# Position biases added by VectorE, and 128-fold bias tables, in a three-block fp32 transformer kernel

## The reference, cut to what matters

```python
# block 1 (one layer): gated linear attention + block attention + convolutional FFN
proj = rmsnorm(x) @ w_in                     # qa ka va ra a_lr | qb kb vb | gates
oa = rmsnorm(gla_chunked(qa, ka, va, log_sigmoid(a_lr @ w_lr_up + b_forget) / 16)) * g * silu(ra)
logits = qb @ kb.T / 8 + rel_bias[t5_bucket(q_pos - k_pos)]      # 8 heads of 64
ob = softmax(where(k_pos <= q_pos, logits, -inf)) @ vb
mixed = g_a * (oa @ w_branch_gla) + g_b * (ob @ w_branch_moba)   # g = sigmoid(gates)
x = x + mixed @ w_out;  x = x + conv_swiglu(rmsnorm(x))
# block 2: stick-breaking attention and pooling, attention on a memory, then
logits = rmsnorm(x) @ w_router + b_router    # 32 experts
top4 = top_k(logits, 4); gates = softmax(top4)
x = x + sum over the 4 experts e of gate_e * (clamped_swiglu(h @ w1[e] + b1[e]) @ w2[e] + b2[e])
# block 3, two layers: l0 = sparse + differential attention with a T5 bias; l1 = the last:
logits = q @ k.T / 8 + table[clip(q_pos - k_pos)]                # 16 heads of 64
masked to the own chunk of 64 tokens and those before it; softmax; @ v
# each layer also: two half-step SwiGLU FFNs, attention on a memory; at the end rmsnorm
```

## Time and profile before

| | |
|---|---|
| median of three runs | 3231.62 us |
| the profiled execution | 3234.32 us, span 3232.5 us |
| PE busy | 3057.5 us (95%) |
| PEld busy | 2186.9 us (68%) |
| DVE busy | 781.9 us (24%) |
| ACT busy | 514.7 us (16%) |
| POOL busy | 12.5 us |
| DMA | 723.01 MB, mean 224 GB/s |

### The profile page before, as it was taken

The page is one execution under the profiler, slowest core; times in us unless marked ns, Lnnn a source line. Parts: engine busy times, 40 slices in busy tenths (PEclk is TensorE's granted clock), DMA queues, the critical chain, the costliest instruction groups (busy, mean ns, idle before and its releaser), DMA issues.

```text
span 3232.5 us, 34397 instructions
## 1 busy us (share of the span) xinstructions
PE 3057.5 (95%) x14190; PEld 2186.9 (68%) x14190; DVE 781.9 (24%) x1766; ACT 514.7 (16%) x1014; POOL 12.5 (0%) x21
## 2 busy tenths in 40 slices
PE   7999999999899998989988999989999999989999
PEld 5788888768443433433433888767888888857887
DVE  1131441332211111111111311454210210443210
ACT  2120320121111111111111100123200100132100
POOL 0000000000000000000000000000000000000000
PEclk9999999999899999999999999999999999998999
DMA  7333444323699999999999344532344444532341
GB/s 281 115 123 130 182 157 156 133 102 110 256 429 428 429 428 429 428 429 428 428 429 428 141 156 161 189 119 79 131 150 146 173 150 145 200 117 79 142 148 62
DMA packets 52217, 723.01 MB, mean 224 GB/s; under 512 B 5692, under 2 KB 5692, under 8 KB 8336
## 3 DMA queue, kind: packets, MB, share of 16 engines
q1 hardware_dynamic: 48672, 705.73, 54.7%
q0 software_dynamic: 3440, 15.74, 1.4%
HBM read 720.32 MB, written 1.12 MB: 223 GB/s over the span
## 4 chain that ended last, share of the span: by engine, by line
PE 79%; DMA 17%; DVE 2%; ACT 1%; issue 1%; SPq 0%; ACTq 0%; POOL 0%; DVEq 0%; POOLq 0%
PE ps L518 66%; DMA sb_a<-stream 9%; DMA sb_weights<-stream 8%; PE ps L1104 5%; PE ps L1126 4%; PE ps L1046 2%; PE ps L1081 2%; PE ps L777 1%; DVE sb_squares L1656 0%; ACT sb_squares L1346 0%; DVE sb_a L2176 0%; ACT sb_o L1278 0%; ACT sb_tr L1278 0%; ACT sb_ex L1346 0%; PE ps L1141 0%
## 5 line engine op out<-in xcount | busy, mean ns | idle before, releaser
L518 PE MATMUL ps<-sb_h,sb_weights 128*128 128x256 f32 x5328 | 1167.7, 381 | 29.1 <-DMA sb_weights<-stream 17.7
L518 PEld LDWEIGHTS ps<-sb_h,sb_weights 128*128 128x128 f32 x5328 | 1013.7, 191 | 173.2 <-issue 29.9
L1104 PE MATMUL ps<-sb_weights,sb_k 128*64 128x512 f32 x1792 | 461.8, 609 | 30.3 <-DMA sb_weights<-stream 26.7
L518 PE MATMUL ps<-sb_a,sb_weights 128*128 128x256 f32 x2016 | 438.9, 380 | 3.2 <-DVE sb_a L1910 3.2
L518 PEld LDWEIGHTS ps<-sb_a,sb_weights 128*128 128x128 f32 x2016 | 383.8, 191 | 56.3 <-DVE sb_a L1910 3.6
L1104 PEld LDWEIGHTS ps<-sb_weights,sb_k 128*64 128x64 f32 x1792 | 144.0, 140 | 316.9 <-issue 280.3
L1126 PE MATMUL ps<-sb_weights,sb_k 128*64 128x512 f32 x768 | 236.6, 614 | 52.7 <-DMA sb_a<-stream 28.9
L2070 DVE TENSOR_TENSOR sb_v<-ps,sb_small 128x256 f32<-128x256 f32 x128 | 48.4, 420 | 666.6 <-PE ps L1071 666.6
L1126 PEld LDWEIGHTS ps<-sb_weights,sb_k 128*64 128x64 f32 x768 | 72.4, 141 | 193.7 <-issue 193.7
L518 PE MATMUL ps<-sb_o,sb_weights 128*128 128x256 f32 x768 | 172.1, 386 | 7.9 <-DVE sb_o L1658 4.2
L1752 DVE TENSOR_TENSOR sb_ex<-ps,sb_rstd 128x512 f32<-128x512 f32 x88 | 60.9, 692 | 482.6 <-PE ps L518 482.4
(11 more groups left out here) (282 smaller groups left out, 1889.1 us busy)
## 6 DMA issues: line engine op xcount, KB each, us to landing
sb_weights<-stream SPq DMA_DIRECT2D x303, 2048.0 KB, 12.4
sb_a<-stream SPq DMA_DIRECT2D x32, 2048.0 KB, 18.3
sb_a<-tables POOLq DMA_DIRECT2D x2, 2048.0 KB, 17.8
sb_a<-tables POOLq DMA_DIRECT2D x2, 1536.0 KB, 15.2
sb_a<-tables POOLq DMA_DIRECT2D x2, 1024.0 KB, 10.7
sb_h<-mem POOLq DMA_DIRECT2D x2, 1024.0 KB, 5.1
sb_small<-small SPq DMA_DIRECT2D x1, 1390.0 KB, 9.4
sb_x<-x SPq DMA_DIRECT2D x1, 1024.0 KB, 4.8
```

Of the source, the lines that this page charges most:

```text
L518: ins = pe.matmul(out, lhsT, rhs, start=start, stop=stop, skip_group_check=skip)
L1104: ins = pe.matmul(ps[own[e], :], XG[:, k * PAIR + e * LOT:k * PAIR + (e + 1) * LOT], w[e][:, k * 512:(k + 1) * 512], start=k == 0, stop=k ...
```

## The change

1. *Biases by VectorE* (`added`, for `moba` and `band`): TensorE's bias matmuls are left out. DVE adds the bias tile from `A` to the PSUM logits, writes the sum to `ex(h)`, and takes the maximum there; this add frees the bank. ScalarE's exponentials run in place. DVE waits for the turning of head h-4, ScalarE no longer frees a bank but raises a semaphore of its own.
2. *Tables*: tables 0 and 2 are stored 128 times over (`wide_tables`), by a DMA whose source repeats each partition's row; they are loaded with a row step one less than a row, which gives the keys unreversed. Table 1 stays. For the last layer the masks' halves change over, and DVE, not PE, waits for them.
3. *w_out*: each sum stands right behind its product, and PE waits for each one as it comes to it.
4. *Router*: the bias row goes first, in two halves; the late sums stand between the token halves of the logits and leave out the sum over features; DVE's clearing stands in `router_begin`, both token halves advance together; the first h copy comes before the exponentials. `b_down` and the gates go into the lots' own buffers, so that pair 0's spread does their product; four matmuls with zeros open banks 4 to 7.
5. *Spread and the last pair*: `spread` moves behind the first chunk of a pair; pair 15 moves out of the loop behind the branch on PE, ACT, DVE and SP.
6. *Start*: SP loads the gains (169 columns of `small`), x, chunk 0, the constants, the rest of `small`, chunks 1 to 4, and the engines wait for what they need.

```diff
@@ SP's start
+            sp.dma_start(small[:, 0:ALL_GAINS], small_d[:, 0:ALL_GAINS]).then_inc(sem("gains_loaded"), 16)
             sp.dma_start(X[:, :], x_d).then_inc(sem("x_loaded"), 16)
+            load(0, 0, W[0][:, :])
             sp.dma_start(const[:, :], const_d).then_inc(sem("const_loaded"), 16)
-            sp.dma_start(small[:, :], small_d).then_inc(sem("small_loaded"), 16)
-            for c in range(SLOTS):
+            sp.dma_start(small[:, ALL_GAINS:], small_d[:, ALL_GAINS:]).then_inc(sem("small_loaded"), 16)
+            for c in range(1, SLOTS):
@@ POOL: stores and loads of the tables
-                pool.dma_start(tables_d[i, 0:n, :], src).then_inc(sem("tables_stored"), 16)
+                if i == 1:
+                    pool.dma_start(tables_d[i, 0:n, :], src).then_inc(sem("tables_stored"), 16)
+                else:
+                    pool.dma_start(wide_d[i // 2, 0:n, :, :], src.unsqueeze(1).broadcast_to([n, P, TAB])
+                                   ).then_inc(sem("tables_stored"), 16)
             pool.wait_ge(sem("tables_stored"), 48)
...
+                        src = bass.AP(tensor=wide_d.tensor, offset=(i // 2) * 16 * P * TAB + 2 * P - 1 - P * t,
+                                      ap=[[TAB - 1, P], [P * TAB, n], [1, T]])
@@ PE: softmax_pairs
-                        for e in range(2):
+                        for e in range(0 if "added" in a else 2):
@@ DVE: softmax_pairs
-                        maxima(b, h, True)
+                        if "added" in ATT[name]:
+                            if h >= 4:
+                                banks.wait_filled(dve, (name, "turned", h - 4))
+                            if h == 2:
+                                squares_free(dve, before)
+                            for t in range(2):
+                                cols = keys(True, t)
+                                ins = dve.tensor_tensor(ex(h)[:, cols], PS[b][:, cols], A[:, h * 512:(h + 1) * 512][:, cols], ALU.add)
+                            ins.then_inc(banks.emptied[b], 1)
+                            banks.wait_emptied(dve, (name, "logits", h))
+                            for t in range(2):
+                                ins = dve.tensor_reduce(stat("max", h)[:, t:t + 1], ex(h)[:, keys(True, t)], AX_X, ALU.max)
+                            link(ins)
...
                     for h in (2 * p - 2, 2 * p - 1) if 1 <= p <= n else ():
-                        banks.wait_emptied(dve, (name, "logits", h))
+                            dve.wait_ge(sem(f"{name}_exps"), h + 1)
@@ DVE and PE: w_out
-            for i in range(4):
-                banks.wait_emptied(dve, ("branch_a", i))
-                banks.wait_emptied(dve, ("branch_b", i))
-                dve.tensor_tensor(tile(GATES, 2 * i, 2), tile(GATES, 2 * i, 2), tile(GATES, 8 + 2 * i, 2),
-                                  ALU.add).then_inc(sem("mixed"), 1)
+                    if g:
+                        banks.wait_emptied(dve, ("branch_a", i))
+                        banks.wait_emptied(dve, ("branch_b", i))
+                        dve.tensor_tensor(tile(GATES, 2 * i, 2), tile(GATES, 2 * i, 2), gate, ALU.add
+                                          ).then_inc(sem("mixed"), 1)
-            pe.wait_ge(sem("mixed"), 4)
-            down("w_out", tiles(GATES, 8))
+            down("w_out", tiles(GATES, 8), ready=lambda k: pe.wait_ge(sem("mixed"), k // 2 + 1))
@@ PE: router and experts
-                    mm(PS[b][:, t * E:(t + 1) * E], h[k][:, t * P:(t + 1) * P], S("w_router", k * E, (k + 1) * E),
-                       k == 0, k == KT - 1)
-            mm(PS[b][:, 2 * E:3 * E], ones[0:1, :], S("b_router")[0:1, :], True, True).then_inc(banks.filled[b], 1)
-            late_sums("n_moe")
+                    ins = mm(PS[b][:, t * E:(t + 1) * E], h[k][:, t * P:(t + 1) * P], S("w_router", k * E, (k + 1) * E),
+                             k == 0, k == KT - 1)
+                if t == 0:
+                    late_sums("n_moe")
+            ins.then_inc(banks.filled[b], 1)
...
+            for i in range(4):
+                b = banks.begin(pe, ("moe", i), 4 + i)
+                mm(PS[b][:, 0:1], ones, ZERO[:, 0:1], True, False, True)
...
-            for m in range(KT):
-                mm(PS[4 + m // 2][:, (m % 2) * T:(m % 2 + 1) * T], V[0:E, m * P:(m + 1) * P], GATE_T,
-                   m % 2 == 0, False, True)
...
-                spread()
                 for fill in GATHERED:
...
+                    else:
+                        spread()
...
-            with pe.Fori(0, E // 2) as i:
+            with pe.Fori(0, LAST_PAIR) as i:
                 pair(i, first_lots)
...
+            pair(LAST_PAIR, first_lots)
...
             spread(last=True)
```

More of the change, by code:

```diff
@@ L41 @@
 MORE_LOTS = T * TOP // LOT
+LAST_PAIR = E // 2 - 1
 TAB = 512
@@ L382, in build @@
         ATT = {
[L383 removed]
+            "moba": dict(causal=True, added=True, heads=8, dh=64, bias=0, q=lambda h, t: [half(Q, 4, h, t * P, P)],
                          k=lambda h: [half(K, 4, h)], v=lambda h, s: V[:, s * 1536 + 1024 + 64 * h:s * 1536 + 1088 + 64 * h],
@@ L618, in tm, with down @@
                             between[2 * c + t]()
-            def down(name, src, before={}, between={}):
+            def down(name, src, before={}, between={}, ready=lambda k: None):
                 n = len(src)
@@ L999, in _ @@
             begin_norm("n_moe")
+            b = ring_bank("router_bias")
+            for half_ in range(2):
+                ins = mm(PS[b][:, half_ * 16:half_ * 16 + 16], ones[0:1, :], S("b_router", half_ * 16, half_ * 16 + 16)[0:1, :],
+                         True, True)
+            ins.then_inc(banks.filled[b], 1)
             norm_done(pe, "n_moe")
@@ L1150, in results_copied @@
                     pe.wait_ge(L.emptied[b], n * PAIR_FILLS[b] + L.base[b])
-            with pe.Fori(0, E // 2) as i:
+            with pe.Fori(0, LAST_PAIR) as i:
                 pair(i, first_lots)
[L1154 to L1157, removed]
+            results_copied(first_lots, LAST_PAIR)
             pe.wait_ge(sem("counted"), 1)
@@ L1176, in _ @@
                 results_copied(more_lots, MORE_LOTS // 2)
+            pair(LAST_PAIR, first_lots)
+            for b in range(4):
+                banks.skip(b, PAIR_FILLS[b] * (E // 2))
+            chunk[0] += MOE_CHUNKS * E
+            results_copied(first_lots, E // 2)
             spread(last=True)
@@ new lines, in _ @@
+            dve.wait_ge(sem("chosen"), 2)
+            dve.wait_ge(sem("router_exp"), 2)
+            for t in range(2):
+                ins = dve.tensor_tensor(gates[t], chosen[t], GATE_EXP[:, t * E:(t + 1) * E], ALU.mult)
+            link(ins)
+            for t in range(2):
+                ins = dve.tensor_reduce(ST[:, 26 + t:27 + t], gates[t], AX_X, ALU.add)
+            link(ins)
+            link(dve.reciprocal(ST[:, 26:28], ST[:, 26:28]))
+            for t in range(2):
+                dve.tensor_scalar(gates[t], gates[t], ST[:, 26 + t:27 + t], None, ALU.mult).then_inc(sem("gates_ready"), 1)
@@ L2339, in _ @@
             pool.dma_start(O[:, :], mem3_d).then_inc(sem("n_mem3_loaded"), 16)
-            for i in range(4):
-                banks.wait_filled(pool, ("mem2_o", i))
-            pool.dma_start(V[0:E, 0:D], b_down_d).then_inc(sem("b_down_loaded"), 16)
+            pool.wait_ge(sem("spread_cleared"), 1)
+            pool.dma_start(Y_TOK[0:E, :], b_down_d).then_inc(sem("b_down_loaded"), 16)
             for l in ("l0", "l1"):
```

157 lines of the change are left out of this document (98 added, 59 removed).

## The result

The changed kernel takes 3275.5 us at the median of four runs (3272.68 to 3279.68), against 3233.98 before (four runs). The ratio is 1.0132, 95% interval 1.0112 to 1.0152: slower by 41.5 us, where 26 were forecast, and 0.5 us beyond the range.

A forecast was written before the change was run, and what follows sets the result against it. TensorE was taken to bound the kernel outside the experts, a full DMA stream inside them. Terms +51 - 5.1 - 4.0 - 12.4 - 4.1 + 1.4 = +26.8 us gave 3261 us profiled, 3258 at the median; range 3199 to 3275.

The forecast's parts named there:

- not slowed: Rival on the wide table stores: they run at full rate and land by 85, total 3203 us; chance 0.20.
- half-slowed one: Rival on the wide table stores: 43 us in all, TensorE 8.5 us late, total 3217 us; chance 0.13.
- start and tables, to block 1's attention: Stores of 84 us make VectorE, then TensorE, 49.3 us late, start's gain included, plus 2 for the clock: +51 us.
- block 1's attention: First block's biases on VectorE: three pairs of heads gain 1.4 us each, the fourth 0.9: -5.1 us.
- w_out: Branch sums between products: TensorE starts w_out 2.2 us earlier and keeps its clock, 1.8 us: -4.0 us.
- router to the first expert matmul: Reordered router, b_down's product moved into pair 0's spread: first expert matmul earlier, all kept: -12.4 us, bounds 8 and 15.
- experts, last pair: Last pair behind the branch: 8.4 us saved at the last spread, last pair ending 4.3 us later: -4.1 us.
- last attention: Last layer's biases on VectorE: 4.9 us won by the fills' end, then lost without fills: +1.4 us, bounds -6 and +8.
- 0.7 at the clock: Last layer, steps without fills: 0.7 us lost at the clock, beside the three steps' losses.
- 4.9 us are won by then: Last layer to the end of the fills: shorter steps, and TensorE no longer waiting for the masks, win 4.9 us.
- 2.3, 2.1 and 1.2: Last layer: us lost in three steps without fills, where values start 5.5 us after the turning instead of 3.3.
- The return from the pause: TensorE comes back from the stores' stall at clock 0.5; the steady spread's 3.46 us take 5.80 so: 2 us.

The follow-up runs named there:

- x1: Changed kernel with tables 1 and 2 exchanging buffers, table 1 stored first, VectorE waiting for that store alone before clearing TR: 3214.01 us, 0.9947 of before.
- x3: Changed kernel with the last layer's biases on TensorE again and table 2 stored once, table 0 still 128-fold: 3226.95 us, 0.9986 of before.
- x4: Changed kernel with block 1's biases on TensorE again and table 0 stored once, table 2 still 128-fold: 3238.32 us, 1.0011 of before.
- x10: Changed kernel with the wide stores reading every fourth partition, still 8 and 16 partitions, VectorE's wait kept: 3229.22 us, 0.9987 of before.
- x2: Changed kernel with tables 0 and 2 produced on and stored from all 128 partitions, same bytes, VectorE's wait kept: 3212.1 us, 0.9933 of before.
- x9: x1 with the last layer's biases for pairs 0, 5, 6 and 7 on TensorE, pairs 1 to 4 on VectorE: 3206.38 us, 0.9915 of before.
- x5: x1 with the last pair of experts in the loop again and the branch behind it: 3214.5 us.
- x6: x1 with spread at the head of each pair again: 3215.72 us.
- x12: x1 with a product of zeros of b_down's size put back between the turning of the gates and the gather: 3221.43 us, 0.9965 of before.

## Why the prediction was wrong, point by point

**The mechanism and the direction held.** Stores forecast at 84 us from 60.3 on, landed at 144.6; they landed at 146.3. TensorE was to stand from 93 to 147.1; it stood from 92.1 to 148.9. x1 shows that this wait is the whole loss, x3, x4 and x10 that the rate is the source partitions'. The case "not slowed" was wrong; so was the half-slowed one. That 50 GB/s came so near to the measured 51 is in part luck: it rested on one store of eight pieces, and 55 ns of its 0.33 us were a guess. The stores took from 58.6 to 146.3, 87.7 us instead of 84, and began 1.7 us earlier than forecast.

The Trainium skill, SBUF — State Buffer, "Door 1: The DMA port swizzle", gives four neighbouring partitions, and the four that lie 32 further, one port of about 27 GB/s; by it the estimate for the stores is 77 us. The runs agree with its mechanism: 51 and 103 GB/s from two and four groups of four neighbours, and 195 to 205 in x10, where by its rule sixteen partitions and eight both have eight ways out. The Trainium skill, DMA: Bandwidth & Descriptors, "Anatomy of one DMA", takes a fixed 2 us and the bytes at 436 GB/s; by it the estimate for the 4 MB store is 11.6 us. From partitions 0 to 15 it took 86.8 us, and from 128 (x2) 22.9, beside other traffic, so the bytes alone do not price it here.

The sum was +26.8, measured +38.4, term by term in the profiled pair:

| term | forecast | measured |
|---|---|---|
| start and tables, to block 1's attention | +51 | +55.4 |
| block 1's attention | -5.1 | -5.3 |
| w_out | -4.0 | -3.8 |
| half clock behind a pause at 742 us | 0 | +1.0 |
| router to the first expert matmul | -12.4 | -14.4 |
| experts, last pair | -4.1 | -1.6 |
| block 3 to the last attention | 0 | 0.0 |
| last attention | +1.4 | +7.1 |

**The step that failed is the last layer**, half of the miss (+1.4 forecast, +7.1 measured), and in it mostly one term: "0.7 at the clock" was about 5.6. Two parts of it. First, "4.9 us are won by then", the end of the fills: measured is 2.1. The steps with a fill did gain, 3.9 us in all. But I had TensorE no longer wait for the masks; the wait is still in its program, VectorE's was added (what stands ahead of the prediction has this wrong too), and 1.36 us of idle time before 2873.88 show it. Nor did I see that without the bias matmuls TensorE only arrives earlier at the scaling of the memory by ScalarE, waits 4.04 us for it, and runs the first fill partly at half clock: 9.99 us instead of 7.14. So the way from the start to the first turning became 1.8 us longer (17.9 for 16.1), and 3.9 less 1.8 is the 2.1.

Second, "2.3, 2.1 and 1.2" for the steps without a fill: measured 2.83, 3.18 and 3.19, with the clock in them. The clock can be taken out by the rows. At half clock VectorE's add begins 1.01 us after the turning (2932.27), at full clock 0.65 (2924.24); the next turning begins 1.48 us after the values (2931.26), before the change 0.80 (2899.26). That is 0.68 us in the first of these steps and 1.04 in the other two, 2.8 in all. What is left is 2.15 in each of the three. So the chain (add, maximum, negate for both heads one after the other, exponentials, copies) was priced right in the first two steps; it repeats whole in the third, where I let it fade to 1.2. x9 gave back 8.4 us by leaving those steps to TensorE; it removes the longer chain and the half clock together, so it does not part them.

**The return from the pause** is the second: "2 us" for the clock, measured 4.3. I priced one stretch of 16 matmuls. Behind the pause 16 matmuls took 5.65 instead of 2.6 us and the projection after them 15.31 instead of 14.08. In x3 (pause 15.1), x4 (16.2) and x10 (11.2) the 16 matmuls took 5.66, 5.65 and 5.65: the length of the pause made no difference to them. The projection behind took 15.4 us in x3 and x10, but 16.8 in x4; why is open. The stall proper, 148.94 against 97.8, was 51.1 us instead of 49.3.

**The experts**: -4.1 forecast, -1.6 measured, but x5 and x6 show that this stage scatters by 4 us with the same code, so the term is neither confirmed nor refuted.

**The router** brought 2 us more than forecast; x12 shows some 6 of the 14.4 in b_down's product alone (26.9 us from the router's first matmul to the first expert matmul, 21.0 in x1). **w_out** and **block 1** were right to 0.2 us. **The start** brought 6.4 us instead of 4.7 (first matmul 17.7 to 11.3).

The remaining 3 us between the profiled pair (+38.4) and the medians (+41.5) are scatter: the profiled run was the fastest of the changed kernel's four.

## What to carry to other kernels

Before a DMA out of SBUF, count the partitions it reads and how they lie; a replicating store from a few neighbouring rows runs at a fraction of the rate while the DMA share looks full. Ask of each store which buffer it holds and who overwrites that next: here one moved wait and two exchanged buffers turned +1.3% into -0.5%. Work taken off the busiest engine pays only in steps where the other engine's chain is covered; price the uncovered steps one by one, and with them the half clock that the new gaps bring.

## What the runs showed of the hardware

- Replicating stores in 4 KB packets: 51 GB/s from 8 neighbouring partitions, 103 from 16, 195 from 16 that lie four apart (8 of them giving to both stores), 205 when only those 8 were left, 368 from 128. At 51 and 103 the packets' time filled 0.48 and 0.96 of the engines, at 205 it filled 0.50.
- A small store queued behind a wide one waits for it: table 1's 24 KB took 45.9 us to land in the changed kernel, 1.8 us in x1, where it goes first.
- From the first expert matmul to block 3 all thirteen kernels took 939 to 946 us. From block 3 to the last attention the same code took 1058 to 1068 us, in two groups: 1058.4 to 1060.1 in the six kernels whose granted clock was 0.93 from 400 to 450 us behind block 3's start (the changed kernel, 1059.8, among them), 1063.0 to 1068.0 in the seven where it was 0.86 (x1 1063.1, x4 1066.3, x9 1068.0). That moves totals by up to 8 us between kernels; x9 lost 4.9 there against x1, more than the 3.9 that it lacks to its theory. What sets it stays open.
